# High and low parts in the two halves of one operand, in the attention heads of a 1-core decoder trunk

## The reference

```python
# layer 0: 12 heads of 64, three (window, dilation) patterns, ALiBi, merged by their softmax denominators
q, k, v, qm = jnp.split(x @ a_w_in, [768, 1536, 2304], axis=-1)
mix = dilated_attention(q, k, v)          # the kernel: one softmax over 1024 keys, log(count) in the bias
# both layers: 4 heads of 64 against the memory's 256 tokens
mk, mv = jnp.split(mem @ w_mem_kv, 2, axis=-1)
s = jnp.einsum('bshd,bmhd->bhsm', qm, mk) * (64 ** -0.5)
p = jax.nn.softmax(s, axis=-1)
mo = jnp.einsum('bhsm,bmhd->bshd', p, mv)
y = jnp.concatenate([mix, mo], axis=-1) @ w_out
x = layer_norm(DN_ALPHA * x + y, ln_mix_g, ln_mix_b)
x = layer_norm(DN_ALPHA * x + (jax.nn.silu(x @ w_gate) * (x @ w_up)) @ w_down, ln_ffn_g, ln_ffn_b)
```

## Time and profile before

| | |
|---|---|
| median of 3 runs | 2523.28 us |
| span of the profiled execution | 2518.2 us |
| TensorE busy | 2393.0 us (95%), 12120 matmuls |
| VectorE busy | 1058.1 us (42%), 2027 instructions |
| ScalarE busy | 519.3 us (21%), 1069 instructions |
| POOL busy | 1056.4 us (42%) |
| mean granted TensorE clock | 0.984 |
| memory pairs, layer 0 | about 28 to 123 us of the span |
| dilated pairs | about 123 to 543 us, 73.2 us each in the loop |
| memory pairs, layer 1 | about 1413 to 1483.5 us |

### The profile page before, as it was taken

The page is one execution under the profiler, slowest core; times in us unless marked ns, Lnnn a source line. Parts: engine busy times, 40 slices in busy tenths (PEclk is TensorE's granted clock), DMA queues, the critical chain, the costliest instruction groups (busy, mean ns, idle before and its releaser), DMA issues.

```text
span 2518.2 us, 31661 instructions
## 1 busy us (share of the span) xinstructions
PE 2393.0 (95%) x12120; PEld 2031.8 (81%) x12120; DVE 1058.1 (42%) x2027; ACT 519.3 (21%) x1069; POOL 1056.4 (42%) x498
## 2 busy tenths in 40 slices
PE   7999999999889999999999898999899999999997
PEld 6888888888678888888887788877688888888885
DVE  5455444466742222222225735556822222222226
ACT  4344433331300000000003532212200000000002
POOL 4311122263754444444443775423854333344443
PEclk9999999999999999999999999999999999999998
DMA  4111001131021111111111021211021111111111
GB/s 152 43 43 42 25 16 42 59 109 59 17 67 50 50 50 50 50 50 50 45 47 42 26 72 47 68 34 34 17 77 49 42 50 50 50 50 50 50 34 67
DMA packets 160453, 127.41 MB, mean 51 GB/s; under 512 B 11520, under 2 KB 146304, under 8 KB 160384
## 3 DMA queue, kind: packets, MB, share of 16 engines
q1 hardware_dynamic: 147808, 114.31, 14.8%
q10 hardware_dynamic: 12576, 12.16, 1.6%
HBM read 122.26 MB, written 4.19 MB: 50 GB/s over the span
## 4 chain that ended last, share of the span: by engine, by line
PE 78%; DVE 10%; issue 7%; ACT 3%; POOL 1%; DMA 0%; DVEq 0%; ACTq 0%; POOLq 0%
PE ps L254 26%; PE ps L255 25%; PE ps L256 25%; DVE XTl L758 2%; PE ps L402 1%; DVE XR L845 1%; DVE st L782 1%; DVE XR L693 1%; ACT mP L497 1%; DVE PTl L582 1%; ACT PTh L506 1%; DVE V L1112 1%; PE ps L651 0%; ACT dP L497 0%; DVE VSl L1129 0%
## 5 line engine op out<-in xcount | busy, mean ns | idle before, releaser
L243 POOL TENSOR_TENSOR Wh<-raw,zcol 128x1024 fp32r<-128x1024 f32 x190 | 366.0, 1926 | 1246.2 <-PE ps L256 968.5
L254 PE MATMUL ps<-XTh,Wh 128*128 128x512 f32 x1760 | 691.3, 393 | 15.2 <-DVE hid L959 9.2
L255 PE MATMUL ps<-XTl,Wh 128*128 128x512 f32 x1760 | 688.3, 391 | 0.0
L256 PE MATMUL ps<-XTh,Wl 128*128 128x512 f32 x1760 | 687.9, 391 | 0.0
L246 POOL TENSOR_TENSOR Wl<-raw,Wh 128x1024 fp32r<-128x1024 f32 x190 | 474.2, 2496 | 14.9
L254 PEld LDWEIGHTS ps<-XTh,Wh 128*128 128x128 f32 x1760 | 332.6, 189 | 84.3 <-DVE XTl L758 15.7
L256 PEld LDWEIGHTS ps<-XTh,Wl 128*128 128x128 f32 x1760 | 332.5, 189 | 69.8
L255 PEld LDWEIGHTS ps<-XTl,Wh 128*128 128x128 f32 x1760 | 332.8, 189 | 67.8
L693 DVE TENSOR_TENSOR XR<-XR,ps 128x512 f32<-128x512 f32 x416 | 281.5, 685 | 228.6 <-PE ps L256 228.6
L959 DVE TENSOR_TENSOR hid<-silu,ps 128x512 f32<-128x512 f32 x88 | 60.4, 686 | 691.5 <-PE ps L256 691.5
L254 PE MATMUL ps<-Wh,hidh 128*128 128x512 f32 x704 | 277.3, 394 | 24.1 <-DVE XR L691 15.4
(11 more groups left out here) (164 smaller groups left out, 2855.8 us busy)
## 6 DMA issues: line engine op xcount, KB each, us to landing
raw<-in_w_gate SPq DMA_DIRECT2D x44, 512.0 KB, 3.8
raw<-in_w_up SPq DMA_DIRECT2D x44, 512.0 KB, 3.8
raw<-in_w_down SPq DMA_DIRECT2D x44, 512.0 KB, 3.7
raw<-in_a_w_in SPq DMA_DIRECT2D x20, 512.0 KB, 5.1
raw<-in_w_out SPq DMA_DIRECT2D x16, 512.0 KB, 3.8
raw<-in_b_w_in SPq DMA_DIRECT2D x14, 512.0 KB, 3.8
dB<-in_c_bias SPq DMA_DIRECT2D x12, 512.0 KB, 3.7
raw<-in_w_mem_kv SPq DMA_DIRECT2D x8, 512.0 KB, 3.8
```

Of the source, the lines that this page charges most:

```text
L243: nc.gpsimd.tensor_tensor(Wh[:, slot, :], raw[:, turn, :], zcol[:, 0:1].to_broadcast([P, UNIT]), ALU.add).then_inc(high_done, 1)
L254: nc.tensor.matmul(dst, wh, xh, start=first, stop=False)
L255: nc.tensor.matmul(dst, wh, xl, start=False, stop=False)
L256: return nc.tensor.matmul(dst, wl, xh, start=False, stop=last)
```

## The change

The zero halves are used. The queries' high part is copied into both halves of `Qh` (new ScalarE copies, semaphore `q_again`), the low part stays in its own half with zeros in the other. The keys become one operand for each head: `K0` and `K1` hold that head's high part in its own 64 partitions and its low part in the other 64. Two matmuls give the scores: `Qh` against K is high times (high + low), `Ql` against K is low times high. The values `Vs` hold for each head the high part in its own 64 columns and the low part in the other 64; two matmuls, against `PTh` and `PTl`, give a 128-row output whose two halves have to be added. Each head has its own half of the bank, so ScalarE copies one half of each output across (`o_copy`), VectorE adds (`halves`), and only then the transposed reciprocals can be written into the same bank (`recip`, moved behind the next step's value block) and multiplied (`mix`, moved one step on). The key eviction is split by head, and there are fewer memsets.

```diff
     class DilBuf:
-        Vh = at("dVh", [P, NT, 192], F32R, A_XR + 16 * KB)
-        Vl = at("dVl", [P, NT, 192], F32R, A_XR + 22 * KB)
+        Vs = at("dVs", [P, NT, 2, P], F32R, A_XR + 16 * KB)
...
-        RSb = at("dRS", [P, 2 * P], F32, A_XR + 29 * KB)
+        Ob = at("dOb", [P, 2 * P], F32, A_XR + 29 * KB)
+        Os = at("dOs", [P, 2 * P], F32, A_XR + 30 * KB)
...
+    def own(hd):
+        return slice(HD * hd, HD * hd + HD)
+    def other(hd):
+        return own(1 - hd)
...
# qk_act
+            for hd in range(2):
+                act.wait_ge(*g("q_high", pi * 4 + 2 * h + hd + 1))
+                nc.scalar.activation(bf.Qh[other(hd), hd, h * 512:h * 512 + 512],
+                                     bf.Qh[own(hd), hd, h * 512:h * 512 + 512].bitcast(F32),
+                                     ACT.Copy).then_inc(g("q_again"), 1)
...
-            nc.scalar.activation(Kh[:, h * 512:h * 512 + n], bank(b, n), ACT.Copy).then_inc(g("k_high"), 1)
+            for hd in range(2):
+                nc.scalar.activation((K0, K1)[hd][own(hd), h * 512:h * 512 + n], bank(b, n)[own(hd), :],
+                                     ACT.Copy).then_inc(g("k_high"), 1)
# qk_dve
-            nc.vector.tensor_tensor(Kl[:, cs], bank(b, n), Kh[:, cs].bitcast(F32), ALU.subtract).then_inc(g("k_low"), 1)
+            for hd in range(2):
+                K = (K0, K1)[hd]
+                dve.wait_ge(*g("k_high", 2 * (pi * nh + h) + hd + 1))
+                nc.vector.tensor_tensor(K[other(hd), cs], bank(b, n)[own(hd), :], K[own(hd), cs].bitcast(F32),
+                                        ALU.subtract).then_inc(g("k_low"), 1)
# pair_pe
-                mm = three(dst, bf.Qh[:, hd, q0], bf.Ql[:, hd, q0], Kh[:, ks], Kl[:, ks], True, True)
+                K = (K0, K1)[hd][:, ks]
+                nc.tensor.matmul(dst, bf.Qh[:, hd, q0], K, start=True, stop=False)
+                mm = nc.tensor.matmul(dst, bf.Ql[:, hd, q0], K, start=False, stop=True)
...
-            dst = bank(6 + c % 2, 2 * P)
+            dst = bank(6 + c % 2, 2 * P, 256 * hd)
             for k in range(nk):
-                mm = three(dst, bf.Vh[:, lo + k, HD * hd:HD * hd + P], bf.Vl[:, lo + k, HD * hd:HD * hd + P],
-                           PTh[:, i % 2, k, :, :], PTl[:, i % 2, k, :, :],
-                           hd == 0 and first and k == 0, hd == 1 and last and k == nk - 1)
+                nc.tensor.matmul(dst, bf.Vs[:, lo + k, hd, :], PTh[:, i % 2, k, :, :], start=first and k == 0, stop=False)
+                mm = nc.tensor.matmul(dst, bf.Vs[:, lo + k, hd, :], PTl[:, i % 2, k, :, :], start=False,
+                                      stop=last and k == nk - 1)
             mm.then_inc(g("pv"), 1)
-            if hd == 1 and last:
-                pe.wait_ge(*g("rden_wide", pi * 4 + c + 1))
-                for q in range(2):
-                    mm = nc.tensor.transpose(bank(6 + c % 2, P, 256 + q * P), ...)
-                mm.then_inc(g("rden_turned"), 1)
+        def recip(c):
+            pe.wait_ge(*g("rden_wide", pi * 4 + c + 1))
+            pe.wait_ge(*g("summed", pi * 4 + c + 1))
+            for q in range(2):
+                mm = nc.tensor.transpose(bank(6 + c % 2, P, q * P), ...)
+            mm.then_inc(g("rden_turned"), 1)
...
+        pe.wait_ge(*g("q_again", (pi + 1) * 4))
         pe.wait_ge(*g("q_low", (pi + 1) * 4))
         scores(0)
...
             if i >= 1:
                 pv(i - 1)
+                if its[i - 1][4] and its[i - 1][0] % 2 == 0 and s >= 3:
+                    recip(s // 2 - 1)
         if fill:
             fill[0]()
         pv(NI - 1)
-        for f in fill[1:]:
+        for f in fill[1:2]:
+            f()
+        recip(3)
+        for f in fill[2:]:
             f()
# pair_act: o_copy(c) stands where rden_copy(c) stood
-            act.wait_ge(*g("rden_turned", pi * 4 + c + 1))
-            nc.scalar.activation(bf.RSb[:, :], bank(6 + c % 2, 256, 256), ACT.Copy).then_inc(g("rden_copied"), 1)
+            act.wait_ge(*g("pv", pi * NI + item_of(kind, 2 * c + 1) + 1))
+            for hd in range(2):
+                nc.scalar.activation(bf.Ob[own(hd), :], bank(6 + c % 2, 256, 256 * hd)[other(hd), :],
+                                     ACT.Copy).then_inc(g("o_copied"), 1)
# pair_dve
+        def halves(c):
+            dve.wait_ge(*g("o_copied", 2 * (pi * 4 + c + 1)))
+            for hd in range(2):
+                ins = nc.vector.tensor_tensor(bf.Os[own(hd), :], bank(6 + c % 2, 256, 256 * hd)[own(hd), :],
+                                              bf.Ob[own(hd), :], ALU.add)
+            ins.then_inc(g("summed"), 1)
         def mix(c):
-            dve.wait_ge(*g("rden_copied", pi * 4 + c + 1))
-            nc.vector.tensor_tensor(dst(pi, c), bank(6 + c % 2, 256), bf.RSb[:, :], ALU.mult).then_inc(g("mixed"), 1)
+            dve.wait_ge(*g("summed", pi * 4 + c + 1))
+            dve.wait_ge(*g("rden_turned", pi * 4 + c + 1))
+            nc.vector.tensor_tensor(dst(pi, c), bank(6 + c % 2, 256), bf.Os[:, :], ALU.mult).then_inc(g("mixed"), 1)
...
             if last and s % 2 == 0 and s >= 2:
-                mix(s // 2 - 1)
+                halves(s // 2 - 1)
             if last and s % 2 == 1:
+                if s >= 3:
+                    mix(s // 2 - 1)
                 rden_of(s // 2)
# start of attention: the zeros
-            for q in (bf.Qh, bf.Ql):
-                nc.vector.memset(q[HD:P, 0, :].bitcast(F32), 0.0).then_inc(g("cleared"), 1)
-                nc.vector.memset(q[0:HD, 1, :].bitcast(F32), 0.0).then_inc(g("cleared"), 1)
+            for hd in range(2):
+                nc.vector.memset(bf.Ql[other(hd), hd, :].bitcast(F32), 0.0).then_inc(g("cleared"), 1)
...
-            for v in (bf.Vh, bf.Vl):
-                nc.vector.memset(v[:, :, HD:2 * HD].bitcast(F32), 0.0).then_inc(g("cleared"), 1)
```

More of the change, by code:

```diff
@@ L113, in build @@
         RB = at("mRB", [P, 2, 2, HD], F32, A_WH + 21 * KB)
-        RSb = at("mRS", [P, 2 * P], F32, A_X + 16 * KB)
+        Ob = at("mOb", [P, 2 * P], F32, A_X + 16 * KB)
+        Os = at("mOs", [P, 2 * P], F32, A_X + 17 * KB)
         zero = at("mzero", [P, M], F32, A_WH + 22 * KB)
@@ L345, in qk_act @@
             for hd in range(2):
-                r = slice(HD * hd, HD * hd + HD)
+                r = own(hd)
                 nc.scalar.activation(bf.Qh[r, hd, h * 512:h * 512 + 512], bank(b)[r, :], ACT.Copy,
                                      scale=QSCALE).then_inc(g("q_high"), 1)
+            for hd in range(2):
[3 more added lines that the diff above has]
+                                     ACT.Copy).then_inc(g("q_again"), 1)
         else:
             n = M if kind == "mem" else 512
-            nc.scalar.activation(Kh[:, h * 512:h * 512 + n], bank(b, n), ACT.Copy).then_inc(g("k_high"), 1)
+            for hd in range(2):
+                nc.scalar.activation((K0, K1)[hd][own(hd), h * 512:h * 512 + n], bank(b, n)[own(hd), :],
+                                     ACT.Copy).then_inc(g("k_high"), 1)
     def qk_dve(dve, kind, pi, j):
@@ L439, in pair_pe @@
         values(0)
[L440 removed]
+        pe.wait_ge(*g("k_low", (pi + 1) * 2 * nh))
+        pe.wait_ge(*g("q_again", (pi + 1) * 4))
         pe.wait_ge(*g("q_low", (pi + 1) * 4))
@@ L490, in v_high @@
             for hd in range(2):
-                nc.scalar.activation(bf.Vh[:, 4 * j:4 * j + m, 2 * HD * hd:2 * HD * hd + HD],
-                                     src[:, :, hd, :], ACT.Copy).then_inc(g("v_high"), 1)
+                nc.scalar.activation(bf.Vs[:, 4 * j:4 * j + m, hd, own(hd)], src[:, :, hd, :],
+                                     ACT.Copy).then_inc(g("v_high"), 1)
         def exp(n):
@@ L531, in pair_act @@
             if last and s % 2 == 0 and s >= 2:
-                rden_copy(s // 2 - 1)
+                o_copy(s // 2 - 1)
         if fill:
             fill[0]()
-        rden_copy(3)
+        o_copy(3)
         for f in fill[1:]:
@@ L550, in v_low @@
             for hd in range(2):
-                vs = (slice(None), slice(4 * j, 4 * j + m), slice(2 * HD * hd, 2 * HD * hd + HD))
-                ins = nc.vector.tensor_tensor(bf.Vl[vs], src[:, :, hd, :], bf.Vh[vs].bitcast(F32), ALU.subtract)
+                ts = slice(4 * j, 4 * j + m)
+                ins = nc.vector.tensor_tensor(bf.Vs[:, ts, hd, other(hd)], src[:, :, hd, :],
+                                              bf.Vs[:, ts, hd, own(hd)].bitcast(F32), ALU.subtract)
             ins.then_inc(g("v_low"), 1)
@@ L629, in pair_dve @@
             fill[0]()
+        halves(3)
+        for f in fill[1:2]:
+            f()
         mix(3)
-        for f in fill[1:]:
+        for f in fill[2:]:
             f()
```

17 lines of the change are left out of this document (7 added, 10 removed).

## The result

The changed kernel takes 2568.34 us (median of 4 runs, 2564.41 to 2571.89) against 2522.65 for the kernel before in the same comparison: a ratio of 1.0184, 95% interval 1.0170 to 1.0199. The direction was as forecast, the size was not: 2534.5 had been predicted, 2548 as the high end. The profiled execution has a span of 2568.3 us, 50.1 more than before.

The account below looks back on a forecast made before the run. The loops were taken as a ring of VectorE, ScalarE and TensorE. Memory pairs +12.8, dilated -2.8, layer 1 start +1.25: +11.2 us on 2518.2, span 2529.4, median 5.1 above: 2534.5 us; range 2508 to 2548.

Parts of the forecast that it names:

- Sizes of the added instructions: Per summed pair of tiles, 0.75 us for two ScalarE copies and 0.91 for two VectorE additions, without overlap.
- rival 1: The 64-partition copies and additions overlap, each even step 0.3 us cheaper: +2 us, 2525.5; chance 0.20.
- The memory ring: Memory pair loop, set by VectorE and ScalarE from the fourth step: net +2.8 us for each of three pairs.
- The walk: Step-by-step delays against before: memory pair 3.0 us late at its last even step, dilated pair -0.7 us.
- The odd step's 0.35: In a memory pair, the odd step after an even one gets the moved multiplication, 0.35 us longer.
- The first even step: Memory pair's third step: waits shrink with fewer matmuls, so it costs only the additions, 0.6 us late.
- The last memory pair's open end: Layer 1's second memory pair, no projection behind it: end takes 2.85 us instead of 1.32; pair 4.4 us longer.
- The dilated pair: Eight-step loop gives back 0.2 us, last item 0.48: -0.7 us each for five, +0.8 for the sixth.
- rival 5: TensorE's clock falls in half-idle memory loops: about 0.5 us a step, 16 us over four, 2550; chance 0.03.
- rival 3: TensorE sets the end, so all 69.8 us of removed matmul work are gained: 2453.5 us; chance 0.04.
- Rival 2: VectorE becomes the bound and all its waits in the dilated loop go: -25 us, 2498; chance 0.13.
- Rival 4: Dilated loop already VectorE's and ScalarE's, TensorE's saving gives nothing: +3.3 us a pair, +35, 2558; chance 0.12.

Follow-up runs that it names:

- e4: Kernel before with only the values' half of the change (two matmuls a block, halves copied and added); scores keep three matmuls: 2559.9 us.
- e7: Kernel before with the change in the four memory pairs alone, the six dilated pairs as before: 2550.7 us.
- e1: Changed kernel with the saved matmuls put back as dead work ahead of score groups and of value blocks of each step's first item: 2566.5 us.
- e6: Changed kernel with the sum of the output halves moved behind the first score pass of the following odd step, nothing added or removed: 2550.9 us.
- e10: Kernel before with the change in the six dilated pairs alone, in its own order, the memory pairs as before: 2536.1 us.
- e5: Changed kernel with five dead 256-wide matmuls behind each step's value block in the memory pairs, where TensorE waits anyway: 2562.8 us.
- e9: Kernel before with the change in dilated pairs alone, sums placed where VectorE waits anyway, reciprocals turned one item later: 2521.7 us.
- e11: e9 with six dead 256-wide matmuls in step 5 and six at the end of step 6 of each dilated pair: 2516.4 us.
- e2: Kernel before with the third product of scores and values left out, no copies or additions added: 2499.5 us.
- e12: e6 with five dead matmuls behind each value block of the memory pairs: 2550.5 us.

## Why the prediction was wrong

**Sizes of the added instructions: right.** Two copies 0.78 us (0.75 said), two additions 0.86 (0.88 to 0.91), the second copy of the queries 1.27 for two (1.26). The halves do not overlap, so rival 1 falls. The trace agrees with the rule of the Trainium skill that the prediction weighed (VectorE: DVE Perf Modes, Two Vector instructions with no wait between them): 0.86 us for the two, 0.42 for one.

**The memory ring: right mechanism, mis-sized.** The walk was 3.0 us late at step 6, which with step 7's multiplication (0.35) is 3.35 at the last reciprocal. Values alone, at full clock, measured 17.2 - 12.97 = 4.2; the changed kernel 5.4. By two steps: 0.95, 1.29 and 1.1 were walked, 1.31, 1.50 and 1.42 measured in e4. The odd step's 0.35 was right (2.12 to 2.46). The even one grew by 1.18: the wait by 0.54 and not by 0.38, and from the start of the additions to the next pass it is 1.00 and not 0.91. The first even step, which I let lose only 0.6 since waits there would take in the rest, lost nearly as much as the others. That is 0.9 us a pair over the walk, some 3.5 for four. The 1.2 us that the changed kernel has on top of e4 lie in steps 2-3 (7.05) and 6-7 (5.19); its window from 90 to 100 us has a part at the low level. The miss in the memory pairs is 15.1 us in all (29.1 against 14.0), so most of it lies elsewhere. With the change in the memory pairs alone (e7), and from one pair's c = 0 to the next one's, the first took 5.8 us more than before, the second (up to the first dilated pair) 6.9, the first of layer 1 9.1, where 2.8 had been walked for each; the last took 5.2 more to its c = 3 and 2.5 behind it, where 4.4 had been walked; and 2.0 lie ahead of layer 1's first c = 0, where 1.25 had been. The largest of these stands where e7 has 31 us at the low level from 1430 to 1540, and the kernel before none.

**The last memory pair's open end** took 3.51 us from the start of the last value matmul to the next work, where it was 1.44 before (1.32 from the transposes behind it, which is what the prediction counted) and 2.85 forecast:

```profile
1529.31 0.41 PE L439 MATMUL ps<-PTl,mVs 128*128 128x256 f32 x1
...
1529.76 0.78 ACT L542 ACTIVATE mOb<-ps 64x256 f32<-64x256 f32 x2 [2.31 <-PE ps L439]
1530.57 0.42 DVE L641 TENSOR_TENSOR mOs<-ps,mOb 64x256 f32<-64x256 f32 x1 [1.16 <-ACT mOb L542]
...
1531.58 0.66 PE L448 MATMUL ps<-ident,mRB 128*128 128x128 f32 x2 [1.85 <-DVE mOs L641]
1532.34 0.42 DVE L648 TENSOR_TENSOR MO<-ps,mOs 128x256 f32<-128x256 f32 x1 [0.91 <-PE ps L448]
...
1532.82 0.58 PE L254 MATMUL ps<-Wh,XTh 128*128 128x256 f32 x1 [0.59 <-DVE MO L648]
```

The links are those of the sum. The value matmuls and the transposes are at the low clock (the transposes 0.66, 0.41 at full clock), and the last addition began 0.43 after the first and ended at 1531.4.

**The dilated pair: the step that failed.** The walk had -0.7 us; the pairs of the hardware loop measured +1.0 to +1.9. The step of the prediction that failed is the one that took TensorE's clock at 1.00 throughout: the sum has no term for it, and rival 5 had a chance of 0.03. What the five pairs show, in the same distances as above:

| dilated pairs, changed kernel | steps 2-3 | 4-5 | 6-7 | rest | sum |
|---|---|---|---|---|---|
| before, each of the five | 7.54 | 12.60 | 11.35 | 41.72 | 73.2 |
| first pair | 8.41 | 12.28 | 13.50 | 40.22 | 74.4 |
| second | 9.76 | 12.28 | 12.01 | 40.19 | 74.2 |
| third | 9.00 | 12.27 | 13.10 | 40.68 | 75.05 |
| fourth | 8.97 | 12.28 | 13.04 | 40.74 | 75.0 |
| fifth | 8.98 | 12.27 | 12.98 | 40.80 | 75.0 |

The granted clock is 1.00 in steps 2-3 of the first pair and in steps 6-7 of the second. Put together from those (8.41, 12.28, 12.01, 40.19), a pair that never loses the clock would take 72.9 us, 0.3 less than before, and the walk had -0.7. That is an estimate from the rows of this table; none of these five pairs is at full clock throughout. By it the ring's part of the walk was nearly right, and the clock costs 1.3 to 2.2 us a pair, 9 us over the five.

By steps: 4-5 measured -0.33 (about -0.5 walked). At steps 6-7 +0.4 was walked; +0.66 came at full clock, as in all five pairs of e1, and +1.63 to +2.15 with a stretch at 1.2 GHz behind TensorE's own waits. At steps 2-3 +0.48 was walked; +0.87 came at full clock, +1.43 to +2.22 in the others. There I had the first low part 0.8 us earlier and "as before" for the score pass behind the additions. In the third pair the first low part came 1.87 us behind c = 0, and 1.81 before, since TensorE's transposes for it ran at 1.2 GHz; seven of them there, and the next seven at full clock:

```profile
305.37 1.70 PE L422 MATMUL ps<-ident,dP 128*128 128x128 f32 x7
...
309.13 0.93 PE L422 MATMUL ps<-ident,dP 128*128 128x128 f32 x7
```

In the first pair it came at 1.20. The rest of the miss at this place is the copies': ScalarE starts them behind the exp of 512 and ended them 4.12 us behind c = 0 in the first pair, where the walk had 3.7, and VectorE waited 1.09 us for them. With the sum moved (e6) the third to fifth pairs lost 1.4 of it at steps 2-3, where the first low part is at 1.2 us too, and 1.0 at 6-7, all of which the clock can account for. The window of one dilated pair, against the first of the earlier trace rows, shows both sides:

```profile
219.10:293.50 74.40, 65.70 (x362) 55.06 (x361) 40.43 (x122) 36.57 (x83) 12.87 (x6) 0.98 0.13 35
```

TensorE's listed work fell by 5.2 of the 9.1 us, VectorE's rose by 6.0 and ScalarE's by 5.7, and the pair is 1.2 us longer. The walk had +2.8 us for three sums and trusted that waits would take them in; at full clock they nearly did. The sixth pair, outside the loop, had +0.8 in all. With the change in the dilated pairs alone (e10) it was 1.8 us late at its c = 3 and lost 3.5 more up to layer 1's first reciprocal: 1.8 in the open end, and the projection behind that begins at 1.2 GHz (a 512-wide matmul every 0.43 us from 554.33).

**Rival 5, the clock, was the right idea with the wrong place and chance.** I gave it 0.03, priced it inside the loop only (0.5 us a step), and argued that gaps of 0.4 and 0.7 us had left the clock at 1.00. Gaps of 0.84, 1.04 and 1.14 us together with fewer matmuls did not. Inside the memory loop it costs little: steps 4-5 took 6.12 in the changed kernel and in e5, at full clock in both, and steps 6-7 with a low part 5.19 against 4.97. The cost is behind it, in the projections, where TensorE is the only engine that counts, and at steps 2-3 and 6-7 of the dilated loop. Shown by a run each are some 4 to 8 us in the memory pairs (e5) and 5 us in the version of e9 (against e11); the 9 us in the dilated pairs of the changed kernel are the estimate above. How much of the 45.7 it is in all was not isolated.

**Rivals 2, 3 and 4.** e2 shows that a saving of TensorE's work alone yields 21 us and not 69.8, so rival 3 was never there. Rival 2 (2498) would have needed the additions to be free. Rival 4 put +3.3 us on a dilated pair; it measured 1.0 to 1.9, and the memory pairs, which I had at +12.8 and +1.25 for the start, gave +29.

In sum: memory pairs 29.1 against 14.0 forecast, dilated pairs 14.8 against -2.8. Two terms failed. The memory ring was under-sized by 0.9 us a pair at full clock, and its open end by 0.5, part of that at the low clock. And TensorE's clock, which I had asked about and put at a chance of 0.03, fell in and behind both kinds of loop; for the dilated pairs that, and not the additions, turned a small gain into a loss.

## What to carry to other kernels

In a ring of three engines the price of an added instruction is set by its place in the queue: the same two additions cost 0.8 us more per double step of a memory pair ahead of a score pass than behind it, and over all pairs 17.5 us with what came back of the clock. Put new work behind the instruction that the next engine waits for. And where matmuls are removed from a loop that waits for other engines, read the granted clock of the work behind the loop as well: TensorE's saving is only worth its share of the path (here 21 of 70 us), and thinning it out can slow down what comes next. To tell the two apart, look for an instance of the same loop body that happens to stand at full clock, and compare it with its neighbours.

## What the hardware did unexpectedly

- Dead matmuls made a kernel faster: 12 a dilated pair, 2521.7 to 2516.4 us, with the granted clock of the profiled executions up from 0.976 to 0.978; filled memory loops moved the window behind the first of them from 0.72 (68 to 76 us) to 1.00 (66 to 76).
- TensorE at 1.2 GHz set in at the end of a stretch with many waits and lasted into full work behind it: 8 us with TensorE busy throughout had 0.72 (68 to 76 us), behind a stretch with 4.86 of 8 us busy, whose last 2 us were at 0.50 already.
- The clock's low stretches move: e6 had none in the third to the fifth dilated pair, e12, which up to there differs only in dead work in the memory pairs, more than 150 us earlier, had one in each of them.
- Of the kernel e6, three runs had a clock of 0.972 to 0.974 and 2547 to 2552 us, and one 0.964 and 2562.3.
